# One-block norms by quarters, and the first branch half of the sample's last attention block loaded within it

## The reference, cut to what matters

```python
h = rms_norm(x, norm1_g) * (1 + sc1) + sh1
z = h @ w_in                     # q, k, v of both attentions, and the gate logits (2 x D)
o_g = gqa_attention(...)         # sample tokens see their own keys and 128 cached ones
o_d = rms_norm(diff_attention(...), subln_g) * (1 - lam_init)
gate_a, gate_b = split(sigmoid(gate_logits))
merged = gate_a * (o_g @ w_branch_a) + gate_b * (o_d @ w_branch_b)
x = x + g1 * (merged @ w_out)
h2 = rms_norm(x, norm2_g) * (1 + sc2) + sh2
x = x + g2 * peer_layer(h2, ...) # queries h2 @ w_query, 8 heads x 16 experts of 16384, rows of u and v gathered
y = rms_norm(x, final_norm_g)
```

## Time and profile before

| | us |
|---|---|
| median of 3 runs | 4969.04 |
| lowest and highest | 4962.42, 4969.89 |
| the profiled execution, its own time | 4963.66 |
| its span in the trace | 4962.0 |

### The profile page before, as it was taken

How to read it: one execution, slowest core, us unless ns; L and a number is a source line. 1 busy time by engine, 2 the same in 40 slices (tenths; PEclk the granted TensorE clock), 3 DMA queues, 4 the chain that set the end, 5 groups by cost and what they waited for, 6 DMA issues and landing times.

```text
span 4962.0 us, 32620 instructions
## 1 busy us (share of the span) xinstructions
PE 3353.4 (68%) x11402; PEld 1282.1 (26%) x11402; DVE 2719.3 (55%) x4132; ACT 450.1 (9%) x824; POOL 1663.8 (34%) x1365
## 2 busy tenths in 40 slices
PE   4979888999699898999998862333333333334334
PEld 0333343444344443444443430000000000000000
DVE  2321129987133202577778888556565656565653
ACT  0011010000122201111010110000000000000000
POOL 0000004443233000344534566544433444344432
PEclk8989999999799999999999985555555555555555
DMA  9988987899899687999999999999999999999998
GB/s 377 389 324 325 368 315 298 335 355 385 321 404 399 251 293 296 354 365 365 365 393 391 378 419 421 408 421 421 421 411 418 422 421 421 415 415 421 421 421 327
DMA packets 407518, 1869.37 MB, mean 377 GB/s; under 512 B 30016, under 2 KB 33632, under 8 KB 238160
## 3 DMA queue, kind: packets, MB, share of 16 engines
q0 software_dynamic: 187200, 1347.98, 66.4%
q1 hardware_dynamic: 220176, 519.60, 28.0%
HBM read 1835.65 MB, written 33.13 MB: 377 GB/s over the span
## 4 chain that ended last, share of the span: by engine, by line
DMA 48%; PE 33%; DVE 11%; issue 6%; POOL 1%; ACT 1%; SPq 1%; DVEq 0%; POOLq 0%; PEldq 0%; ACTq 0%
DMA big<-in_peer_u,sel 25%; PE ps L899 24%; DMA big<-in_peer_v,zt 11%; DMA big<-in_w_in 3%; DMA activations<-in_peer_v,zt 3%; DVE big L1851 2%; DMA big<-in_w_ada 2%; PE ps L999 2%; DMA big<-in_peer_v,zone 2%; PE ps L1059 2%; DVE big L1798 1%; PE ps L1037 1%; DMA big<-in_w_out 1%; PE ps L950 1%; DVE big L2173 1%
## 5 line engine op out<-in xcount | busy, mean ns | idle before, releaser
L899 PE MATMUL ps<-big,activations 128*128 128x512 f32 x4032 | 1781.3, 602 | 87.9 <-ACT zt L1332 26.7
L899 PEld LDWEIGHTS ps<-big,activations 128*128 128x128 f32 x4032 | 769.5, 193 | 1083.4 <-issue 992.6
L2173 DVE CUSTOM_DVE_ANT_0 big<-big,activations 128x2048 f32<-128x2048 f32 x256 | 587.2, 2294 | 500.8 <-DMA big<-in_peer_u,sel 498.1
L1317 PE MATMUL ps<-activations,zt 128*32 128x512 f32 x1528 | 368.4, 1058 | 689.8 <-DMA activations<-in_peer_v,zt 508.2
L1317 PE MATMUL ps<-big,zt 128*32 128x512 f32 x1544 | 358.2, 1021 | 480.8 <-DMA big<-in_peer_v,zt 472.5
L881 POOL DMA_INDIRECT big<-in_peer_u,sel x384 | 423.2, 1102 | 579.7 <-DVE zt L2173 524.9
L2173 DVE CUSTOM_DVE_ANT_0 big<-big,zone 128x2048 f32<-128x2048 f32 x128 | 292.9, 2293 | 210.3 <-DMA big<-in_peer_u,sel 209.7
L850 POOL DMA_INDIRECT big<-in_peer_u,sel x128 | 215.2, 1681 | 286.6 <-DVE zone L1851 251.2
L1851 DVE CUSTOM_DVE_ANT_0 big<-big 128x2048 f32<-128x2048 f32 x128 | 288.8, 2290 | 39.1 <-DMA big<-in_peer_u,sel 37.5
L887 POOL DMA_INDIRECT activations<-in_peer_v,zt x191 | 193.2, 1012 | 335.7 <-PE ps L1317 326.4
L1798 DVE SCALAR_TENSOR_TENSOR big<-big,work 128x2048 f32<-128x2048 f32 x115 | 270.5, 2352 | 58.4 <-DMA big<-in_peer_v,sel 54.5
(11 more groups left out here) (224 smaller groups left out, 2687.7 us busy)
## 6 DMA issues: line engine op xcount, KB each, us to landing
big<-in_w_in SPq DMA_DIRECT2D x84, 2048.0 KB, 11.5
big<-in_w_ada SPq DMA_DIRECT2D x48, 2048.0 KB, 13.4
big<-in_w_out SPq DMA_DIRECT2D x24, 2048.0 KB, 13.9
big<-in_peer_w_query SPq DMA_DIRECT2D x24, 2048.0 KB, 10.4
big<-in_w_branch_a SPq DMA_DIRECT2D x12, 2048.0 KB, 20.1
big<-in_w_branch_b SPq DMA_DIRECT2D x12, 2048.0 KB, 8.0
big<-z_blocks SPq DMA_DIRECT2D x20, 512.0 KB, 9.4
big<-in_peer_u,sel POOLq DMA_INDIRECT x626, 37.5
```

The costliest lines, as they stand in the source:

```text
L899: ins = nc.tensor.matmul(bank(bk), acts[:, k, b * P:(b + 1) * P], w[:, n % WS, k], start=(start and k == 0), stop=(stop and k == KT // 2 - 1))
L1317: ins = nc.tensor.matmul(ps[32 * j:32 * j + 32, q * 512:(q + 1) * 512], spread[(t - 1) % 2][:, k * 32:(k + 1) * 32], v_slot(m)[:, j * CH:( ...
L2173: V.tensor_tensor_reduce(out=x, in0=x, in1=h_of[ph], scale=1.0, scalar=0.0, op0=ALU.mult, op1=ALU.add, accum_out=dots_s[t % 2][:, k:k + 1] ...
```

## The change

1. In the last attention block the early gates run at steps 11 to 15 (4, then 5 a step) in place of 9 to 14; ACT takes the first product out at step 13.
2. The w_a half of chunk 0 of g = 1 is loaded within that block, behind the third early half and ahead of SyncE's wait, into slot (H_BR[1] + 5) % 3 = 2. w_b takes number H_BR[1] + 4 (slot 1) after the block. TensorE still does w_a's product first, and frees both slots together after w_b's.
3. `norm2_rows` is issued after chunk 1's store for g = 0 as before, and for g = 1 after chunk 2's.
4. `residual` also takes the chunk's sum of squares; `scale_row` (A's instruction) follows chunk 2; `norm_rows` does what is left of the norm, its last two steps by quarters of 512 columns, each with a signal of its own.
5. TensorE turns quarters 0 and 1, does the first query half, turns quarters 2 and 3 and does the second.

```diff
--- before.py
+++ after.py
@@ -588,6 +588,7 @@
                     sums_out(SB - 1)
                     for j in range(EARLY_HALVES):
                         if j == 3:
+                            half(H_BR[1] + 5, 0, 0, part(w_a, 0, 0))
                             sp.wait_ge(mm_done, U_BR[1] + 1)
                         at = (0, 1, 2, 1)[j]
                         sp.dma_start(early_w[at], part(w_in, j % 2, ZW + j // 2 * D)).then_inc(early_in[at], 16)
@@ -605,8 +606,8 @@
 
                 if g == 1:
                     sp.wait_ge(att[1]["o"], NB)
-                for j in range(4, 6 if g == 1 else 4):
-                    half(H_BR[g] + j, 0, 0, br(0, j))
+                if g == 1:
+                    half(H_BR[1] + 4, 0, 0, br(0, 5))
                 if g == 1:
                     sp.wait_ge(sum_st, 16 * NQ * NQ)
                     sp.wait_ge(mm_done, U_BR[1] + 2)
@@ -693,6 +694,7 @@
                             sp.dma_start(yp[0], ac(A1 + 2 * D, D)).then_inc(y_out, 16)
                         else:
                             ada_rows(10)
+                    if c == (1, 2, DCH)[g]:
                         norm2_rows()
 
                 for i in range(4 if g < 2 else 0):
@@ -705,7 +707,7 @@
                         if c < DCH - 1:
                             half(H_QRY[g] + 2 * (c + 1) + j if g else RING_AT["qry", 2 * c + 2 + j], 0, 0, part(w_qry, j, (c + 1) * CH))
                     if g == 1 and c == 1:
-                        sp.wait_ge(s["h"], R + 1)
+                        sp.wait_ge(s["h"], 4 * (R + 1))
                         sp.wait_ge(att[1]["st"], 16 * LAST)
                         for lb in range(2):
                             sp.dma_start(o_nat[lb], osd[block_of(2, lb)]).then_inc(grp[2]["nat"][lb], 16)
@@ -1116,8 +1118,8 @@
                         if p:
                             for n in tokens_behind(i, sc):
                                 token(n)
-                            if i == SB - 1 and sc in range(9, 15):
-                                early_gates(4 * (sc - 9), 4 * (sc - 8))
+                            if i == SB - 1 and sc > 10:
+                                early_gates(max(0, 5 * (sc - 11) - 1), 5 * (sc - 10) - 1)
                         else:
                             gate(sc)
                             if sc in (3, 11):
@@ -1160,13 +1162,18 @@
                     if g == 0:
                         ada(A_BR + 2 * c)
                     for p_ in range(2):
-                        nh = first(4 + p_)
+                        turned = g == 1 and early
+                        nh = first(5 - p_ if turned else 4 + p_)
                         wait_half(nh, i, 6)
                         for b in range(n):
                             v = (2 + p_) * n + b
                             pe.wait_ge(bank_free, u + (v + 1 + NB - DEPTH[g]))
                             products(oT[g][:, p_ * (KT // 2):(p_ + 1) * (KT // 2)], b, nh, bk(v), True, True).then_inc(mm_done, 1)
-                        release(u + (3 + p_) * n)
+                        if not turned:
+                            release(u + (3 + p_) * n)
+                        elif p_:
+                            release(u + (3 + p_) * n)
+                            pe.sem_inc(w_free, 1)
                     if g == 0:
                         ada(A_BR + 2 * c + 1)
 
@@ -1199,11 +1206,13 @@
                     if g == 0:
                         ada(A_OUT + c)
 
-                def turned_rows(lb):
-
-                    pe.wait_ge(nrm[g]["h"], R + lb + 1)
-                    transposes(T_H[g] + lb, h_of[lb] if g == 2 else nbuf[g][1])
-                    pe.wait_ge(t_free, (T_H[g] + lb + 1) * 4 + 4)
+                def turned_rows(lb, quarters=range(4)):
+
+                    src = h_of[lb] if g == 2 else nbuf[g][1]
+                    for q in quarters:
+                        pe.wait_ge(nrm[g]["h"], lb + 1 if g == 2 else 4 * R + q + 1)
+                        quarter(T_H[g] + lb, q, src[:, q * CH:(q + 1) * CH])
+                    pe.wait_ge(t_free, (T_H[g] + lb) * 4 + quarters[-1] + 1 + 4)
 
 
                 units = DCH * n
@@ -1245,11 +1254,11 @@
 
                 if g == 2:
                     first_queries()
-                else:
-                    turned_rows(0)
                 for c in range(1 if g == 2 else 0, DCH):
                     nh = H_QRY[g] + 2 * c if g else RING_AT["qry", 2 * c]
                     for h in range(2):
+                        if g < 2 and c == 0:
+                            turned_rows(0, range(2 * h, 2 * h + 2))
                         wait_half(nh + h, 0, 0)
                         for b in range(n):
                             v = c * n + b
@@ -1457,7 +1466,7 @@
                             exps(sc + 2)
                         if p and sc == 10 and i < 2:
                             spread_quarter(i + 2)
-                        if p and sc == 12 and i == SB - 1:
+                        if p and sc == 13 and i == SB - 1:
                             evac(U_BR[1], 7, early_raw[0])
                         if p == 0 and sc == 7:
                             evac(U_BR[0], 5, gate_raw[0])
@@ -2005,6 +2014,21 @@
                     link(V.tensor_tensor(zt[:, v % 4], zt[:, v % 4], zn(c * CH, CH), ALU.mult))
                     dve.wait_ge(G["xt"][lb], 16 * (R + 1))
                     signal(V.tensor_tensor(zt[:, v % 4], zt[:, v % 4], zn(D + c * CH, CH), ALU.add), G["ou"], B * DCH + v + 1)
+                    link(V.tensor_tensor_reduce(out=hcur[:, c * CH:(c + 1) * CH], in0=zt[:, v], in1=zt[:, v], scale=1.0, scalar=0.0,
+                                                op0=ALU.mult, op1=ALU.add, accum_out=small[:, 40 + v:41 + v]))
+
+                def norm_rows():
+
+                    s = nrm[g]
+                    x, h, A, Bv, _ = nbuf[g]
+                    link(V.tensor_reduce(small[:, 2:3], small[:, 40:44], AX.X, ALU.add))
+                    signal(V.tensor_scalar(small[:, 0:1], small[:, 2:3], 1.0 / D, EPS, ALU.mult, ALU.add), nrm_ms, s["base"] + 1)
+                    dve.wait_ge(nrm_rs, s["base"] + 1)
+                    link(V.reciprocal(small[:, 3:4], small[:, 1:2]))
+                    for q in range(4):
+                        at = slice(q * CH, (q + 1) * CH)
+                        link(V.scalar_tensor_tensor(h[:, at], x[0][:, at], small[:, 3:4], A[:, at], ALU.mult, ALU.mult))
+                        signal(V.tensor_tensor(h[:, at], h[:, at], Bv[:, at], ALU.add), s["h"], 4 * R + q + 1)
 
                 def residual_2(v):
 
@@ -2022,8 +2046,8 @@
 
                 def scale_row():
 
-                    dve.wait_ge(nrm[2]["row"], 48)
-                    link(V.scalar_tensor_tensor(nbuf[2][2], nbuf[2][2], 1.0, nbuf[2][4], ALU.add, ALU.mult))
+                    dve.wait_ge(nrm[g]["row"], 48 * (1 + R))
+                    link(V.scalar_tensor_tensor(nbuf[g][2], nbuf[g][2], 1.0, nbuf[g][4], ALU.add, ALU.mult))
 
                 def norm_2(lb):
 
@@ -2057,7 +2081,9 @@
                         residual(v)
                         if g == 0 and v == 2:
                             ada((A_OUT + 2) // 4)
-                    norm(nrm[g], g, 0, T_H[g])
+                        if v == 2:
+                            scale_row()
+                    norm_rows()
                     link(V.memset(acc, 0.0))
                     if g == 0:
                         ada(ADA_PR - 1)
```

## The result

The changed kernel takes 4936.66 us (median, 4 runs from 4928.38 to 4938.19), the kernel before 4968.09 (4 runs by then, 4962.42 to 4969.89). The ratio is 0.9936, 95% interval 0.9921 to 0.9952: faster by 31.4 us (24 to 39 by the interval), where 34.5 were worked out and 4932 was forecast. In the profiled executions the spans are 4962.0 and 4933.5, 28.5 apart.

What follows compares the result with a forecast made beforehand. It took the kernel as a row of stages with different bounds, where idle time at seams (hand-overs between stages) costs its full length. 13.1 + 7.8 + 7.5 + 6.1 = 34.5 us from a mean of 4966.3 gave 4932, range 4920 to 4950.

Steps and rivals of the forecast that it cites:

- eaten later: Sample's projections, paced by DMA, lose g = 0's 6 us; 4956 to 4976 if later stages absorb the rest; chance 0.08.
- smaller gain: Rival for the total: slow clock at the early gates or late rows of g = 1; gain 15 to 28 us; chance 0.17.
- Seam 1: Early gates, last attention block: other work fills TensorE's wait for the load, output(11) starts sooner; gain 6.8 us (3.5 to 7.3).
- ACT's take-out ... costs nothing: Early gates: ACT's step 13 take-out waits for TensorE's step 14 product; its next work is step 15, so cost nothing.
- rival of a slow clock: Early gates: the clock falls as before, costing 3.25 us there and as much in w_a; shares smaller gain's 0.17.
- Seam 2: w_a and w_b behind attention: earlier w_a load shortens the queue, chunk 1 starts sooner; 13.1 us together with Seam 1.
- late release of the two slots: Behind w_b's product: both slots free together, next half nearly on the path; 0.5 us cost at 300 GB/s.
- Seam 3: Output projection of g = 1: later rows let w_out's half land sooner; 8.8 gained, 1.0 lost, net 7.8 us.
- new wait: Output projection of g = 1: scale_row on DVE waits for all three rows, costing 1.0 us.
- Seam 4: Norms: shorter DVE chain and quarters start the query halves sooner; gain 6.1 us in g = 0, 7.5 in g = 1.
- the slow clock spreads: Sign of a wrong prediction: TensorE work beyond the places slow before runs at half rate; no size given for the sign.
- two halves at 7.0: Norms: after the quartered norm each query half takes 7.0 us, first ending at 14.9, second at 23.7 behind residual(3).

Runs made afterwards that it cites:

- The two parts alone: Kernel before with only the gates and w_a load changed, 4954.9 us; with only the norms and moved rows changed, 4946.12 us; kernel before 4965.38.
- gate steps: Changed kernel with gates at 4, 6, 6, 4, 4 instructions a step instead of 4, 5, 5, 5, 5; 4939.84 us, timed once.
- rows back: Changed kernel with g = 1's three rows issued after chunk 1's store, as before the change; 4942.53 us, timed once.
- filler: Changed kernel with extra unread matmuls (4 in g = 0, 6 in g = 1) between output projection and turns; 4929.47 us, ratio 0.9932.
- attention part alone: Kernel before with only the gates moved and the w_a half loaded within the block, norms as before; 4954.9 us, ratio 0.9978.
- gates alone: Kernel before with only the gates two steps on, w_a and w_b both loaded behind the block; 4956.62 us, timed once.
- early half alone: Kernel before with only the w_a half loaded within the block, gates at steps 9 to 14; 4956.48 us, timed once.
- whole norm: Changed kernel with the norm's last two steps in one piece each and all transposes ahead of the first query half; 4941.70 us, timed once.

## Why the prediction was right

**The total.** Forecast 4932, range 4920 to 4950; measured 4936.66. The frame held: a row of stages, each started by the last, so that time taken out at a seam moves everything. The two parts alone, 10.5 and 19.3 us by their medians, add to the whole within its interval. The rival "eaten later" has nothing for it: the stage behind g = 0 is as long with the new norm as with the old (989.6 and 990.2 us), and the last stretch, whose change of length the prediction named as a sign of being wrong, is 6.4 us shorter in this pair of profiles, but not by the change.

The number was closer than its terms. Three of its four terms came out below their own lower bounds: 8.3 against 9.5 for seams 1 and 2, 4.4 and 5.9 against 6.1 for the two norms. With 27.3 us at the seams the gain is at the edge of the rival "smaller gain" (15 to 28), but by neither of its causes: the clock did not fall at seam 1, and the late rows cost 0.5 us.

**Seam 1**, 6.8 worked out, 5.6 measured. The step "ACT's take-out ... costs nothing" failed. ACT indeed lost nothing, but the second gate product goes to the same bank, and its first instruction now lies in the same step as the first product's last, so TensorE waited 0.78 us for ACT. The gate steps show it (O 39.9). Of the 0.4 us that are left, 0.2 are the load, 8.59 in place of 8.38. The rival of a slow clock did not come: the granted clock is 1.00 in 1656 to 1662.

**Seam 2**, 13.1 for seams 1 and 2, measured 11.0 to chunk 1's first product and 8.3 to the end of its first two halves. From w_b's issue at 1699.72 to chunk 1 it was 23.5 us, against 23.4 by the queue of before and 21.9 by bytes alone; the first was right, and the value between them was taken. The step that failed is the clock: chunk 1 was taken at 14.0 us, and behind a wait of 5.64 it took 16.7. The wait had been foreseen, at 4 us, its price had not. The Trainium skill, page "TensorE: Matmul & The Clock Gate", section "HAM oscillation — how this bites in real kernels", has waits for DMA between bursts return the array to half rate. This wait agrees with it (granted clock 0.53 in 1723 to 1729); before, chunk 1 stood behind a wait of 3.60 us and took 14.01, so there the trace does not show it. The 2.7 us are the price in this execution. Five other kernels have the same attention part and waits of 5.46 to 5.75 us there, and their two halves take 15.45 to 16.85 us, so the price is 1.5 to 2.9 and more often near 1.5. The remark that the late release of the two slots would cost 0.5 us at 300 GB/s does not come out of its own terms: 2.1 MB then take 7.0 us, and 1720.5 + 7.0 is just the 1727.5 at which the half is wanted.

**Seam 3**, 7.8 worked out, 8.7 measured. The mechanism was confirmed by putting the rows back (8.1 us). The new wait cost 0.5 in place of 1.0, and TensorE's side gave 9.2 in place of 8.8.

**Seam 4**, 6.1 and 7.5 worked out, 4.4 and 5.9 measured. The DVE chain was right to a tenth (7.9 us to the first product), the turns between the halves to 0.2 (1.6 in place of 1.8). The size that was off is the term "two halves at 7.0": the first took 8.76 and 9.77. For g = 1 half of the slow clock had been taken to go; none did, and g = 0, which had run 14.00 before, got one. So the prediction's own sign of being wrong, that the slow clock spreads, came in part. The filler shows that this is the clock: it alone brings the halves to 7.13. The share of quarters in this seam was overrated: at most 1 us each at the clock as it is, 1.4 at an even one. For g = 1 the "before" is not firm either: of the four kernels with the old norm two have N1 at 32.3 to 32.4 us and two (attention part alone, gates alone) at 29.9 and 29.6, with the same code from there on. So the gain of g = 1's norm is between 3.2 and 7.1 us by these profiles, and 5.9 is that of one pair.

**VectorE's price for pieces.** The rows after show 0.75 and 0.69 us for a 128 x 512 instruction. The four quarters run from 638.49 to 644.51, 6.0 us, where the two whole instructions took 4.7: 1.3 more, signals included. The prediction named 0.9 for it, but its 1.47 us per quarter held 1.2, so the sum did not suffer. The 0.4 that the table of the Trainium skill's page "VectorE: DVE Perf Modes" would give ("The TRN2 errata — SBUF-src ops pay a fixed extra latency per instruction") is too little, and the section itself says that this row of the table under-predicts; its warning that small pieces pay a fixed cost each holds.

The sizes were too large in sum, 34.5 against 27.3 at the seams. The 7.2 us are the slow clock (2.7 in seam 2, and most of 1.7 and 1.6 in seam 4), ACT's wait (0.8), the queue (0.9) and what else seam 1 fell short (0.4), less 0.9 that seam 3 gave more. That the whole run gave 31.4 lies within what its interval leaves open (24 to 39 us), and that it came out nearer to 34.5 than the seams did is chance.

## What to carry to other kernels

Look at a seam between two stages as three things at once: the chain of small instructions, the queue that brings the next weights, and what TensorE's clock will be when it starts again; a chain shortened by quarters gave under 1 us until the pause was filled, and 1.4 then. Order a queue by who needs a transfer first: 3 MB ahead of a 2 MB half that was wanted first cost 8 us in one place and 6 to 7 in another, slow clock included. When a step's work is spread over slots in a loop, put the boundary of a product on the boundary of a slot, or the engine waits for its own result to be taken away.

## What was not expected of the hardware

A shorter pause can cost more behind it than a longer one. With the norm by quarters, TensorE idles 3.1 us (g = 0) or 5.3 to 6.2 (g = 1), does two turns of four transposes and then the query half, which took 8.5 to 9.8 us in all twelve cases (six kernels without filler, two groups), where 7.13 is full speed. With the norm whole it idles 6.4 to 12.3 us and does 16 transposes in 3.3 to 3.7 us at a granted clock of 0.50 to 0.57. Then the two halves ran in 14.00 in eight of ten cases (five kernels, two groups), and in 16.45 in the other two, both in g = 1 (the earlier trace rows and the early half alone). In the eight cases the transposes alone bore the slow clock, 1.4 to 1.7 us of it. With quarters the eight transposes take only 1.8 to 2.2 us, and the product behind them begins at the lower clock, 1.2 GHz (granted 0.50 in 1924 to 1930 of the changed kernel). Which share of it runs there differs from one execution to the next.

Behind waits for DMA ahead of chunk 1 the two halves took 13.99 us after 2.37 us of idle and 14.01 after 3.60, but 15.69 after 3.85, and a single half 8.83 after 3.30. In eight kernels that wait 5.39 to 5.75 us there they took from 15.45 to 16.85, with no order by the wait. The kernel with the rows back has the changed kernel's code up to this place, and waits as long (5.62 against 5.64 us), yet it took 15.45 where the changed one took 16.71:

```profile
1725.61 15.45 PE L901 MATMUL ps<-big,activations 128*128 128x512 f32 x32 [5.62 <-DMA big<-in_w_in]
```

So the same products ran with and without a slow start behind idle times of 3.3 to 3.9 us, and behind one of 5.5 us (whole norm, and filler) they took 15.50 or 16.85: the length of the idle alone does not settle it. What else does was not tried, and a single profile of such a place is good to about 1.5 us.
